# First feed-forward's last block and the mixing memory of a hybrid decoder layer, reordered

## The reference, cut to what matters

```python
h = modulate(rms_norm(x, ln1), sh1, sc1)
x = x + 0.5 * g1 * swiglu(h, w_f1_up, w_f1_down)
h = modulate(rms_norm(x, ln_mix), shm, scm)
u, q, k, v, glr, og = split_in(h @ w_in)
...                     # pooling and gated linear attention
x = x + gm * mix        # mix = concat([z_pool, o]) @ w_out
h = modulate(rms_norm(x, ln2), sh2, sc2)
x = x + 0.5 * g2 * swiglu(h, w_f2_up, w_f2_down)
```

## Time and profile before

| | |
|---|---|
| time, median of 3 runs | 2182.08 us |
| lowest and highest | 2180.16 and 2182.96 us |
| span of the profiled execution | 2175.5 us |
| PE busy | 2099.4 us, 97% of the span |
| DVE busy | 1030.7 us, 47% |
| ACT busy | 551.5 us, 25% |
| POOL busy | 120.1 us, 6% |

### The profile page before, as it was taken

How to read it: one execution, slowest core, us unless ns; L and a number is a source line. 1 busy time by engine, 2 the same in 40 slices (tenths; PEclk the granted TensorE clock), 3 DMA queues, 4 the chain that set the end, 5 groups by cost and what they waited for, 6 DMA issues and landing times.

```text
span 2175.5 us, 31934 instructions
## 1 busy us (share of the span) xinstructions
PE 2099.4 (97%) x12627; PEld 1995.7 (92%) x12627; DVE 1030.7 (47%) x2060; ACT 551.5 (25%) x893; POOL 120.1 (6%) x139
## 2 busy tenths in 40 slices
PE   6899999999999999989999898999999999999997
PEld 3799999999999999888898888999999999999996
DVE  4753344244334324556665775544434442444336
ACT  2521111111211111254545552411121112111213
POOL 2100000000000000111303211100000000000000
PEclk7999999999999999999999998999999999999998
DMA  9413212212321221143342423211111111111102
GB/s 349 132 55 91 74 38 82 77 49 67 96 58 48 87 77 39 40 117 87 97 117 81 114 78 89 65 57 39 58 39 39 57 40 40 42 54 39 58 1 83
DMA packets 204050, 160.15 MB, mean 74 GB/s; under 512 B 5378, under 2 KB 177273, under 8 KB 203977
## 3 DMA queue, kind: packets, MB, share of 16 engines
q1 hardware_dynamic: 203821, 159.16, 24.4%
q10 hardware_dynamic: 164, 0.09, 0.0%
HBM read 153.43 MB, written 5.91 MB: 73 GB/s over the span
## 4 chain that ended last, share of the span: by engine, by line
PE 85%; DVE 7%; ACT 3%; DMA 1%; issue 1%; POOL 1%; SPq 1%; POOLq 0%; DVEq 0%; ACTq 0%
PE bank L380 79%; PE bank L386 2%; DVE tmp L1059 1%; DVE mwl L1044 1%; DMA ai<-in_w_ada 1%; POOL tmp L989 1%; PE bank L605 1%; DVE hl L1079 1%; PE bank L602 1%; DVE xT L1106 1%; DVE yst L1196 1%; SPq L289 1%; PE bank L609 1%; PE bank L395 0%; DMA ws<-in_w_ffn_up 0%
## 5 line engine op out<-in xcount | busy, mean ns | idle before, releaser
L380 PE MATMUL bank<-hh,wh 128*128 128x384 f32 (+1 forms) x2112 | 698.0, 331 | 2.0 <-DVE wl L1044 1.3
L380 PE MATMUL bank<-hl,wh 128*128 128x384 f32 (+1 forms) x2112 | 692.6, 328 | 0.0
L380 PE MATMUL bank<-hh,wl 128*128 128x384 f32 (+1 forms) x2112 | 692.0, 328 | 0.0
L380 PEld LDWEIGHTS bank<-hh,wh 128*128 128x128 f32 x2112 | 397.8, 188 | 38.9 <-issue 36.1
L1133 DVE TENSOR_TENSOR tmp<-tmp,bank 128x384 f32<-128x384 f32 x132 | 70.2, 532 | 735.2 <-ACT tmp L778 735.2
L380 PEld LDWEIGHTS bank<-hl,wh 128*128 128x128 f32 x2112 | 397.8, 188 | 0.4 <-issue 0.2
L380 PEld LDWEIGHTS bank<-hh,wl 128*128 128x128 f32 x2112 | 397.8, 188 | 0.0
L778 ACT ACTIVATE tmp<-bank 128x384 f32<-128x384 f32 x132 | 62.5, 474 | 1201.5 <-PE bank L380 1201.5
L1106 DVE SCALAR_TENSOR_TENSOR xT<-bank,ada,xT 128x384 f32<-128x384 f32 (+1 forms) x552 | 310.7, 571 | 101.2 <-PE bank L380 98.6
L380 PE MATMUL bank<-ah,wh 128*128 128x384 f32 (+1 forms) x1056 | 346.3, 328 | 3.8 <-DVE al L1135 2.3
L380 PE MATMUL bank<-ah,wl 128*128 128x384 f32 (+1 forms) x1056 | 344.6, 326 | 0.0
(11 more groups left out here) (172 smaller groups left out, 1532.5 us busy)
## 6 DMA issues: line engine op xcount, KB each, us to landing
ws<-in_w_ffn_up SPq DMA_DIRECT2D x88, 512.0 KB, 4.7
ws<-in_w_in SPq DMA_DIRECT2D x51, 512.0 KB, 4.0
ws<-in_w_ffn_down SPq DMA_DIRECT2D x44, 512.0 KB, 4.2
aws<-in_w_ada SPq DMA_DIRECT2D x88, 256.0 KB, 2.8
ai<-in_w_ada SPq DMA_DIRECT2D x7, 2048.0 KB, 18.4
ws<-in_w_out SPq DMA_DIRECT2D x24, 512.0 KB, 3.8
out_y_p<-yst SPq DMA_DIRECT2D x8, 512.0 KB, 2.6
xin<-in_x_prompt SPq DMA_DIRECT2D x3, 512.0 KB, 6.4
```

The source lines that it names most:

```text
L380: mm = pe.matmul(out, l(k), r(k), start=(k == 0 and a == 0), stop=(k == depth - 1 and a == 2))
```

## The change

In the last block of the first feed-forward, up 5 goes ahead of the second down group. The squares of norm 3 go from behind up 3 to behind up 2, its ones-sum from inside the second down group to behind up 4 (into bank 5 in place of 7), its parts 0 to 5 from behind that group to behind up 4, and the other four from the third down group to behind the products 9, 11, 13 and 15 of the second. One set of norm coefficients is made behind up 3. The tensors of mixing are laid out anew: `mwh` lies over tiles 2 and 3 of `wh`, `mwl` over tiles 2 and 3 of `wl`, `S0` over the down weights' high parts; two gaps keep these places, and ACT's first high split of mixing waits for the last up in place of the last down product. At the end of mixing, ACT splits tiles 0 and 1 of the second feed-forward after the last unit but one and tiles 2 and 3 after the last one, and waits for the stored states behind these splits, not ahead of them. In the first block of the second feed-forward, everything of norm 8 from its ones-sum on goes one up later (`v = u - which`). SP's and POOL's code is not edited.

```diff
--- before.py
+++ after.py
@@ -174,24 +174,26 @@
         with ExitStack() as mix:
             qs = sb("qs", [P, 2, CMAX], F32, mix)
             ks = sb("ks", [P, 2, CMAX], F32, mix)
+            vtmp = sb("vtmp", [P, CMAX], F32, mix)
+            halo = sb("halo", [P, 4, HALO], F32, mix)
+            sb("gap1", [P, 64], F32, mix)
+            mwh = sb("mwh", [P, 2, 1024], F32R, mix)
+            S0 = sb("S0", [P, 2, NSEQ, DV], F32, mix)
+            E = sb("E", [P, 4, EW], F32, mix)
+            sb("gap2", [P, 224], F32, mix)
+            mwl = sb("mwl", [P, 2, 1024], F32R, mix)
             bs = sb("bs", [P, 2, CMAX], F32, mix)
             t1 = sb("t1", [P, 2, CMAX], F32, mix)
             vs = sb("vs", [P, 3, 512], F32, mix)
             og = sb("og", [P, 4, CMAX], F32, mix)
-            E = sb("E", [P, 4, EW], F32, mix)
             attS = sb("attS", [P, 4, P], F32, mix)
             S = sb("S", [P, 3, 2, DV], F32, mix)
-            S0 = sb("S0", [P, 2, NSEQ, DV], F32, mix)
-            mwh = sb("mwh", [P, 2, 1024], F32R, mix)
-            mwl = sb("mwl", [P, 2, 1024], F32R, mix)
             kdT = sb("kdT", [P, 2 * P], F32, mix)
             rows = sb("rows", [P, 512], F32, mix)
             TA = sb("TA", [P, EW], F32, mix)
             TB = sb("TB", [P, EW], F32, mix)
             wp = sb("wp", [P, 4, P], F32, mix)
             wg = sb("wg", [16, 2 * P], F32, mix)
-            halo = sb("halo", [P, 4, HALO], F32, mix)
-            vtmp = sb("vtmp", [P, CMAX], F32, mix)
             bl = sb("bl", [P, 2, 12], F32, mix)
             dec = sb("dec", [P, 2, 12], F32, mix)
         glr = vtmp
@@ -246,7 +248,7 @@
 
         def norm_bank(q):
 
-            return ps[7] if q >= 3 else ps[4 + q]
+            return ps[5] if q == 3 else ps[7] if q > 3 else ps[4 + q]
 
         def x_rows(t):
 
@@ -273,7 +275,7 @@
         def block_order(which, last):
 
 
-            return (0, 1, 2, -1, 3, 4, -2, 5, -3) if which == 0 and last else (0, 1, 2, 3, 4, 5, -1, -2, -3)
+            return (0, 1, 2, -1, 3, 4, 5, -2, -3) if which == 0 and last else (0, 1, 2, 3, 4, 5, -1, -2, -3)
 
 
         def ada_unit(u):
@@ -424,8 +426,11 @@
                         s = 2 * f + half
                         mm = split_product(bank, whi(s), wlo(s), lambda k: hh[:, k, sl], lambda k: hl[:, k, sl], KT)
                     mm.then_inc(s_up[which], 1)
-                    if first and which == 1 and u == 0:
+                    if first and which == 1 and u == 1:
                         ones_sum(q0 + 2, CHN[2])
+                    if last and which == 0 and u == 4:
+                        pe.wait_ge(s_xacc[0], 24 * (NB - 1) + KT)
+                        ones_sum(3, CHN[0])
                     if adas:
                         if u < 4:
                             if u == 0:
@@ -438,6 +443,8 @@
                         pe.wait_ge(s_wsp, b * 6 + (base + 6))
                     sl = slice(CH0[c], CH0[c] + CHN[c])
                     pe.wait_ge(s_act[which], b * 6 + (2 * c + 2 if which == 0 and last else 4 + c))
+                    if which == 0 and last and c == 1:
+                        pe.wait_ge(n_v, 4)
                     for m in range(KT):
                         n = KT * c + m
                         if not (first and n < 3):
@@ -450,9 +457,6 @@
                         if which == 0 and last and n == 11:
                             pe.wait_ge(s_aevc, NAU)
                             ada_select(ps[7])
-                        if which == 0 and last and n == 15:
-                            pe.wait_ge(s_ada, NAU)
-                            ones_sum(3, CHN[0])
                     if adas and c == 0 and not last:
                         pe.wait_ge(s_aevc, b + (AU_FIRST + 1))
                         ada_select(ps[7])
@@ -783,16 +787,17 @@
                             act.wait_ge(s_down[which], b * 24)
                         for t in (4, 5):
                             split_hi((b, base + t) if not isinstance(b, int) else b * 6 + base + t, t % 3, wh[:, t, :])
-                    if first and u == 0:
+                    v = u - which
+                    if first and v == 0:
                         norm_rsqrt(6 * which + 2, 2)
-                    if first and u < 3:
-                        norm_high(6 * which + 2, 2, LATE[u], LATE[u + 1])
-                    if last and which == 0 and u == 3:
+                    if first and 0 <= v < 3:
+                        norm_high(6 * which + 2, 2, LATE[v], LATE[v + 1])
+                    if last and which == 0 and u == 2:
                         act.wait_ge(s_xacc[0], 24 * (NB - 1) + KT)
                         norm_squares(3, 0)
                     if last and which == 0 and u == 4:
                         norm_rsqrt(3, 0)
-                        norm_high(3, 0, 0, 2)
+                        norm_high(3, 0, 0, 4)
                     if u == (4 if first else 3) and not last:
                         for t in (0, 1):
                             split_hi((b, base + 6 + t) if not isinstance(b, int) else b * 6 + base + 6 + t, t % 3, wh[:, t, :])
@@ -827,8 +832,8 @@
                 ffn(0, W_F1, b, False, False)
             ffn(0, W_F1, NB - 1, False, True)
 
-            norm_high(3, 0, 2, KT)
-            act.wait_ge(s_down[0], 24 * NB)
+            norm_high(3, 0, 4, KT)
+            act.wait_ge(s_up[0], 6 * NB)
             split_hi(W_MIX, W_MIX % NWS, mwh[:, 0, :])
             split_hi(W_MIX + 1, (W_MIX + 1) % NWS, mwh[:, 1, :])
 
@@ -876,12 +881,14 @@
                 if g + 2 < NU:
                     split_hi(W_MIX + g + 2, (W_MIX + g + 2) % NWS, mwh[:, g % 2, :])
                 elif g + 2 == NU:
-
+                    for t in (0, 1):
+                        split_hi(W_F2 + t, (W_F2 + t) % NWS, wh[:, t, :])
+                else:
+                    for t in (2, 3):
+                        split_hi(W_F2 + t, (W_F2 + t) % NWS, wh[:, t, :])
                     act.wait_ge(m_ust, 32)
                     act.wait_ge(g_s0, NSEQ)
                     act.wait_ge(m_st, 64)
-                    for t in range(4):
-                        split_hi(W_F2 + t, (W_F2 + t) % NWS, wh[:, t, :])
                 if kind == "p":
                     name, j, _ = PROJ[u]
                     bank = ps[g % RING]
@@ -1137,15 +1144,21 @@
                     if u == 0:
                         for t in (4, 5):
                             split_lo(b * 6 + (base + t), t % 3, wl[:, t, :], wh[:, t, :])
-                    if first and u < 3:
-                        for part in range(LATE[u] + 2 * (u > 0), LATE[u + 1] + 2):
+                    v = u - which
+                    if first and 0 <= v < 3:
+                        for part in range(LATE[v] + 2 * (v > 0), LATE[v + 1] + 2):
                             norm(6 * which + 2, 2, part)
+                    if last and which == 0 and u == 4:
+                        for part in range(6):
+                            norm(3, 0, part)
                     if u == (4 if first else 3) and not last:
                         for t in (0, 1):
                             split_lo(b * 6 + (base + 6 + t), t % 3, wl[:, t, :], wh[:, t, :])
                     if u == 4 and adas:
                         dve.wait_ge(s_apc, b * KT + KT)
                         ada_sums(ps[7])
+                    if u == 3 and adas and last:
+                        norm_coef(1, 4, R_LNM)
 
                 def down(c):
                     for k in range(KT):
@@ -1155,8 +1168,8 @@
                         if not last and n in (3, 6):
                             t = n // 3 + 1
                             split_lo(b * 6 + (base + 6 + t), t % 3, wl[:, t, :], wh[:, t, :])
-                        if last and which == 0 and 16 <= n < 22:
-                            norm(3, 0, n - 12)
+                        if last and which == 0 and 8 <= n < 16 and n % 2:
+                            norm(3, 0, 6 + (n - 9) // 2)
                         if last and which == 0 and n == 23:
                             split_lo(W_MIX, W_MIX % NWS, mwl[:, 0, :], mwh[:, 0, :])
                         if last and which == 1 and n in (17, 20, 23):
@@ -1165,12 +1178,8 @@
                             ada_store(b + AU_FIRST, ps[7])
                     if adas and last and c == 1:
                         dve.wait_ge(s_ada, NAU)
-                        norm_coef(1, 4, R_LNM)
                         norm_coef(2, 7, R_LN2)
                         half_gain(8)
-                        dve.wait_ge(s_xacc[0], 24 * (NB - 1) + KT)
-                        for part in range(4):
-                            norm(3, 0, part)
 
                 for what in block_order(which, last):
                     if what >= 0:
```

## The result

The changed kernel takes 2185.59 us (median of 14 runs, 2179.98 to 2190.39) against 2181.07 for the one before (14 runs beside it): ratio 1.0019, 95% interval 1.0010 to 1.0028, so 4.5 us slower, and clear of no difference. 2183.5 was forecast, with 2178 to 2188 as range. The profiled execution took 2183.98 us with a span of 2182.2; 1.8 us lie around the span, so the span of before, 2175.5, belonged to an execution quicker than its median, and 1.9 of the 6.7 us between the two spans stand ahead of the edited code.

The account below looks back on a forecast made before the run. The matrix engine, with 85% of the chain of waits, was taken as the bound. -2.0 + 3.4 = +1.4 us on the 2175.5 span made 2176.9; with 6.6 around the span, 2183.5 us, range 2178 to 2188.

Parts of the forecast that it names:

- the sum's own upper bound: Whole kernel: the stages' slow bounds, -0.5 and +4.0, together give +3.5 us.
- the second rival: Down groups of the first feed-forward: clock stays low, 6 to 8 us above forecast, about 2190; chance 0.14.
- The stop at product 11: Second down group, last block: new 4.2 us stop until residual n=8, product starting near 911.9, 1.6 us of clock behind.
- The first mixing product: End of the first feed-forward: comes at 929.1 against 931.07, gaining 2.0 us, bounds 3.0 and 0.5.
- the vector engine's bound: First feed-forward: the vector engine owes 16.8 us from 911.28, so the first mixing product cannot start ahead of 928.1.
- Memory and splits at nothing: Mixing tensors and splits: new places gain only the high split's 1.0 us, already counted; splits at mixing's end cost nothing.
- Up 4: Second feed-forward: stands 6.5 us for norm 8, starts 1.8 us later, 1.6 us of clock behind; stage loses 3.4 us.
- the bound of 4.0: Start of the second feed-forward: largest loss, 4.0 us, if every product of 4 us runs at 1.2 GHz.
- The sum: Whole kernel: -2.0 at the first feed-forward and +3.4 at the second make +1.4 us.
- The first (up 4 does not wait): Second feed-forward: norm chain does not hold up 4, the whole is -6.7 us, 2175.4; chance 0.11.
- The third: Scalar engine: each table switch takes 2 x 1.28 us, product 11 3.8 us later, sum about +5.2, 2187.3; chance 0.05.
- The fourth: First feed-forward: product 11's stop eats all the gain, +3.4 us, 2185.5; chance 0.70 together with the forecast.

Follow-up runs that it names:

- `fill_both`: Changed kernel with needless products in its two new stops, 24 ahead of product 11 and 42 ahead of up 4: 2180.23 us, 0.9993.
- `norm8_back`: Changed kernel with norm 8's ones-sum and steps back at their old places: 2178.13 us, 0.9987.
- `after_again`: Changed kernel unaltered, run once more for a second profile: 2187.70 us.
- `order_alone`: Changed kernel with the old places of the mixing tensors and the old wait of the high split: 2184.21 us, 1.0004.
- `half8`: Changed kernel with norm 8's ones-sum between the halves of up 1 and its other steps at their old places: 2175.58 us, 0.9976.
- `memory_alone`: Kernel before with only the new mixing tensor places, the high split's wait for the last up and the new split order: 2182.92 us, 1.0004.
- `norm8_alone`: Kernel before with only norm 8's ones-sum, Ln/Exp and steps one up later: 2185.70 us, 1.0015.
- `half_both`: Changed kernel, norm 8's sum inside up 1 with old steps, norm 3's inside up 4 with steps ahead of that up's Silu: 2171.10 us, 0.9956.
- `half_both_early_low`: `half_both` with the first low split of mixing behind residual 19 of the last down group instead of 23: 2168.53 us, 0.9940.

## Why the prediction was right, point by point

The time is in the range, 2.1 us above the forecast, and the mechanisms were the named ones; two sizes were off, both by the clock. Part of the agreement is luck. The forecast difference was +1.4 us, and the measured +4.5 is above the sum's own upper bound of +3.5; the range holds it because it was widened for the second rival, and the miss is 2.1 and not 3.1 us because the kernel before came out 1.0 us lower than the median that the forecast started from. Most of the weight (0.72) was on a difference too small to measure and 0.17 on slower; the measured 4.5 us are clear of no difference. The 6.6 us that were taken to lie around the span are 1.8 and a quick profiled execution, which changes no difference.

- **The stop at product 11.** Worked out as 4.2 us, ended by residual 8; it was 4.47 and 4.46, ended by `xT`. With the 1.9 us that the origin had moved, the start of 911.9 becomes 913.8; it was 913.91. The chain runs through the steps that were put on the path, in their order.
- **The first mixing product.** Forecast 2.0 us sooner, it came 0.9 us later in one profile and 0.2 sooner in the other (35.2 and 34.0 against 34.3). The step that was too small is "a new stop of 4.2 us stands where none was, with the 1.6 us of clock behind it": the clock cost 3.3 and 4.6 us there. `fill_both` shows this: with the clock held, the stage ends near the vector engine's bound. So do the five profiles that have this stop without the fill: behind it, 6.5, 6.6, 6.8, 8.9 and 9.1 us of low clock (`norm8_back`, `after_again`, `order_alone`, `half8`, the profile after) went with a stage A of 34.0, 34.0, 34.5, 35.1 and 35.2. The working's other half, "I leave the clock loss there as it was" ahead of mixing, went the other way in one profile (4.4 us for the first unit) and held in the other (6.0).
- **Memory and splits at nothing.** Held for the stops: `memory_alone` has the same stop, `order_alone` one that is 0.3 us longer. But the high split was never on the path to mixing, where the working lets 1.0 us of it go out: before, it began at 927.12 and its first half ended near 928.2, while the low split that needs it had to wait for the last residual until 929.75. It is the new order that makes the stop shorter (2.45 us in `order_alone`). The splits at mixing's end cost nothing (1.19 us of wait ahead of the second feed-forward's first product, before 1.31).
- **Up 4.** Forecast 6.5 us of stop, with up 4 starting 1.8 us later; it was 6.82, and the start of 1403.1, moved by the 1.8 us between the two first products, is 1404.9 against a measured 1404.95. Of the 3.4 us only the clock term was mis-sized, 2.5 to 3.1 instead of 1.6: stage C lost 4.4 to 5.1 us in the five profiles that have this stop, above the bound of 4.0 (by its own terms, 1.8 and half of 4, that bound is 3.8).
- **The sum.** -2.0 + 3.4 = +1.4 was forecast; +0.9 - 1.6 + 4.9 = +4.2 is in the trace, without the rest of mixing, and the runs say +4.5. The -1.6 is luck of that execution; in `after_again` the first mixing unit took 6.0 us as before. The runs also say -2.8 for the first part and +4.8 for the second when each is alone; these miss the +4.5 by 2.5, within what intervals of 0.1% (2 us) on each side leave open.
- **The rivals.** The first (up 4 does not wait) did not happen. The second (low clock through both down groups) happened by a third: 9.1 us, about 22 down products ahead of 922.8 and not 78. That is 12 more than the forecast's 10 and not the 20 more of its point of decision, but with 4.6 us lost for 1.6 it reaches the 3 us that were set beside it; in `after_again`, with 3.3, it does not. The third fell: the chain shows 1.28 us for each load, and the next activation 0.01 us behind it. The Trainium skill, ScalarE: Activation LUTs, section What ACT_TABLE_LOAD costs, has about 2.66 us for a switch with its drain; this case's trace does not agree. The fourth (nothing gained at the first feed-forward, 2185.5) came nearest: stage A and the first mixing unit together are 0.7 us shorter than before in one profile and 0.3 in the other, where 2.0 were forecast.

What stays open is what decides the length of a low stretch: the same stop was followed by 9.1 and by 6.6 us.

## What to carry to other kernels

A step that is moved out of one stop has to be followed to its next reader: here the sum left a 3.1 us stop and its steps became a 6.8 us one three ups later, and the cure was to move the sum by half an up and leave the steps. A long wait of the matrix engine costs more than its length: behind the stops of 4.5 and 6.8 us half of another 4.9 to 9.1 us of low clock was lost, and behind the waits of 0.3 to 1.5 us in these two stages there was none. Needless products in the wait gave that part back. A tensor's new place gains by what may then be issued earlier, not by itself: the places were worth 0.3 us of a stop until the low split was issued four products sooner, which took away the other 2.15 us and cost a wait of 0.50.

## What the runs showed of the hardware that was not expected

Behind the stops of 2.15 to 3.98 us the clock was at 1.2 GHz for 3.0 to 4.7 us, or not at all (behind 2.15 us in the profile after and in `half8`, 2.28 in `norm8_alone`, 2.45 in `order_alone`, 3.00 in `norm8_back`). Behind the stops of 4.5 and 6.8 us it was low for 4.9 to 9.1 us, in every profile that had them, and the shorter of the two had the longer stretches: 6.5 to 9.1 us against 4.9 to 6.1. The rest of mixing, whose products no run changes, took between 417.5 and 429.2 us in the twelve profiles of this study, at a mean granted clock of 0.97 in the shortest and 0.94 to 0.96 in the others:

```profile
938.00:1348.00 410.00, 388.86 (x2467) 357.82 (x2465) 267.11 (x493) 206.10 (x311) 78.52 (x88) 0.97 0.35 96
```

is `half_both`, whose profiled execution was its fastest run (2160.52 us), and

```profile
938.00:1348.00 410.00, 389.22 (x2405) 358.32 (x2404) 263.31 (x481) 203.97 (x311) 78.51 (x88) 0.94 0.34 92
```

is `half_both_early_low`: 62 matrix instructions fewer in the same 410 us. A single profile of this kernel therefore says little of the total to within 5 us, while its stops at product 11, ahead of mixing and at up 4 repeat to 0.02 us.
